# Where the causal mask is added: in the matmul group by TensorE, or in place by VectorE

## What is computed

```python
z = jnp.einsum('bhqd,bhkd->bhqk', qi, k).astype(jnp.float32) * scale
mask = key_pos[None, :] < qpos[:, None]
log_beta = jax.nn.log_sigmoid(z)
log_1m = jnp.where(mask, jax.nn.log_sigmoid(-z), 0.0)
after = lax.cumsum(log_1m, axis=3, reverse=True) - log_1m
a = jnp.where(mask, jnp.exp(log_beta + after), 0.0)
```

## Time and profile before

| | us |
|---|---|
| median of three runs | 1707.56 (1707.22 to 1708.33) |
| the profiled execution | 1705.47 |
| its span | 1703.8 |
| PE busy | 1684.4 (99%) |
| DVE busy | 970.5 (57%) |
| ACT busy | 738.5 (43%) |
| POOL busy | 220.3 (13%) |
| granted PE clock | nine tenths or more in all 40 slices, mean 0.999 |

### The profile page before, as it was taken

One profiled execution on the slowest core, in us unless ns is written; L12 is line 12 of the kernel. 1 busy time (PEld: TensorE's weight loads), 2 busy tenths in 40 slices (PEclk: granted clock), 3 DMA queues, 4 the chain that ended last, 5 costly groups with the idle time before them and its releaser, 6 DMA issues.

```text
span 1703.8 us, 22202 instructions
## 1 busy us (share of the span) xinstructions
PE 1684.4 (99%) x7651; PEld 1391.6 (82%) x7651; DVE 970.5 (57%) x1180; ACT 738.5 (43%) x1033; POOL 220.3 (13%) x204
## 2 busy tenths in 40 slices
PE   7999999999999999999999999999999999999998
PEld 6788888888888888888877888888888888888887
DVE  6787776544555434434658877755545543444344
ACT  5677676433333223223346777763333432232231
POOL 3243221000130000000333233200002100000000
PEclk9999999999999999999999999999999999999999
DMA  6232323333333333333343222223333333333333
GB/s 174 75 93 81 98 63 92 88 93 92 105 92 94 98 99 95 91 98 98 111 120 92 75 86 86 87 68 100 91 98 99 97 93 95 98 98 90 96 98 111
DMA packets 307416, 162.19 MB, mean 95 GB/s; under 512 B 5424, under 2 KB 303528, under 8 KB 307368
## 3 DMA queue, kind: packets, MB, share of 16 engines
q1 hardware_dynamic: 305064, 157.37, 31.5%
q10 hardware_dynamic: 2304, 4.20, 0.7%
HBM read 155.25 MB, written 2.10 MB: 92 GB/s over the span
## 4 chain that ended last, share of the span: by engine, by line
PE 95%; DVE 1%; ACT 1%; DVEq 1%; issue 0%; DMA 0%; POOL 0%; ACTq 0%; SPq 0%; POOLq 0%
PE bank L525 29%; PE bank L529 28%; PE bank L526 28%; PE z L598 2%; PE z L526 1%; PE z L525 1%; PE z L529 1%; PE z L571 1%; PE z L572 1%; PE misc L614 1%; PE misc L612 1%; DVEq L1595 0%; DMA gates<-in_x 0%; DVE w_lo L1192 0%; PE z L576 0%
## 5 line engine op out<-in xcount | busy, mean ns | idle before, releaser
L525 PE MATMUL bank<-xg_hi,w_hi 128*128 128x512 f32 x1584 | 622.7, 393 | 1.3 <-DVE xg_lo L1600 1.3
L526 PE MATMUL bank<-xg_lo,w_hi 128*128 128x512 f32 x1584 | 617.9, 390 | 0.0
L834 ACT ACTIVATE w_hi<-raw 128x1024 fp32r<-128x1024 f32 (+1 forms) x296 | 305.5, 1035 | 558.3 <-DMA raw<-in_w_gate_up 226.9
L1192 DVE TENSOR_TENSOR w_lo<-raw,w_hi 128x1024 fp32r<-128x1024 f32 (+1 forms) x296 | 391.2, 1324 | 38.0 <-ACT w_hi L834 22.1
L529 PE MATMUL bank<-xg_hi,w_lo 128*128 128x512 f32 x1584 | 392.3, 390 | 0.0
L525 PEld LDWEIGHTS bank<-xg_hi,w_hi 128*128 128x128 f32 x1584 | 297.6, 188 | 63.9 <-DVE xg_lo L1600 1.8
L526 PEld LDWEIGHTS bank<-xg_lo,w_hi 128*128 128x128 f32 x1584 | 297.7, 188 | 61.8 <-issue 0.7
L529 PEld LDWEIGHTS bank<-xg_hi,w_lo 128*128 128x128 f32 x1584 | 297.5, 188 | 62.0 <-issue 0.5
L1197 DVE TENSOR_TENSOR S<-bank,rstd 128x512 f32<-128x512 f32 x152 | 104.9, 690 | 269.3 <-PE bank L529 268.7
L525 PE MATMUL bank<-mid_hi,w_hi 128*128 128x512 f32 x480 | 189.9, 396 | 0.0
L526 PE MATMUL bank<-mid_lo,w_hi 128*128 128x512 f32 x480 | 189.6, 395 | 0.0
(11 more groups left out here) (206 smaller groups left out, 1686.7 us busy)
## 6 DMA issues: line engine op xcount, KB each, us to landing
raw<-in_w_in SPq DMA_DIRECT2D x112, 512.0 KB, 3.8
raw<-in_w_gate_up SPq DMA_DIRECT2D x88, 512.0 KB, 3.8
raw<-in_w_down SPq DMA_DIRECT2D x48, 512.0 KB, 3.6
raw<-in_w_branch_out SPq DMA_DIRECT2D x16, 512.0 KB, 3.6
raw<-in_w_o SPq DMA_DIRECT2D x16, 512.0 KB, 3.5
raw<-in_w_branch_out SPq DMA_DIRECT2D x16, 256.0 KB, 2.7
gates<-in_x SPq DMA_DIRECT2D x4, 512.0 KB, 7.1
mix_hi<-yb_hi ACTq DMA_DIRECT2D x8, 256.0 KB, 2.3
```

The source lines that it names most:

```text
L525: mm(dst[:, :], wh[:, k0 + k, :], his[k], start=(k % per == 0), stop=False)
L526: mm(dst[:, :], wh[:, k0 + k, :], los[k], start=False, stop=False)
L834: af(w_hi[at.slot(c)][:, 0:kc, :], raw[at.slot(c)][:, 0:kc, :], ACT.Copy).then_inc(hi_done, 1)
L1192: tt(w[:, 0:kc, :], r[:, 0:kc, :], h[:, 0:kc, :].bitcast(F32), ALU.subtract).then_inc(lo_done, 1)
```

## The change

`scores` no longer runs the three mask matmuls. The last score matmul of each z tensor raises a new semaphore `z_raw`, and a new function `causal` on DVE waits for it, adds `mask_add` to the diagonal columns of z in PSUM and raises `z_done`. `mask_add` is stored as plain fp32.

```diff
-        mask_add = sb("mask_add", [P, P], F32R)
+        mask_add = sb("mask_add", [P, P])
...
                         mm(dst, k_both[:, e, ks], q_twice[:, e, qs], start=(n == 0), stop=False, skip_group_check=True)
-                        mm(dst, k_both[:, e, ks], q_lo[:, e, qs], start=False, stop=False, skip_group_check=True)
-
-                    first = [Z_AT[i] // P for i in blocks]
-                    dst = z[g][:, :].rearrange("p (b q) -> p b q", q=P)[:, first[0]::(first[-1] - first[0]) or NT, :]
-                    mm(dst, ident_r[:, :], mask_add[:, :].rearrange("p (a q) -> p a q", a=1).broadcast_to([P, len(first), P]),
-                       start=False, stop=True, skip_group_check=True).then_inc(z_done, 1)
+                        last = mm(dst, k_both[:, e, ks], q_lo[:, e, qs], start=False, stop=(i == blocks[-1]),
+                                  skip_group_check=True)
+                    last.then_inc(z_raw, 1)
...
+            def causal(h3):
+
+                for g, blocks in Z_BLOCKS:
+                    dve.wait_ge(z_raw, h3 + (g + 1))
+                    first = [Z_AT[i] // P for i in blocks]
+                    diag = z[g][:, :].rearrange("p (b q) -> p b q", q=P)[:, first[0]::(first[-1] - first[0]) or NT, :]
+                    tt(diag, diag, mask_add[:, :].rearrange("p (a q) -> p a q", a=1).broadcast_to([P, len(first), P]),
+                       ALU.add).then_inc(z_done, 1)
+
...
                         yc_add(l * 8 + j * 2, 0)
+                        causal(h3 + 3)
                         softplus_sum(h3 + 3)
...
                     yc_add(l * 8 + j * 2, 0)
+                    causal(h3 + 3)
                     softplus_sum(h3 + 3)
...
                     yc_add(l * 8 + (j * 2 + 1), 1)
+                    causal(h3 + 6)
                     yc_rest(l * 8 + (j * 2 + 1), j, 1)
...
+                causal(l * 24)
                 with dve.Fori(0, PAIRS - 1) as j:
```

More of the change, by code:

```diff
@@ L265, in build @@
         slab_in = sem("slab_in")
+        z_raw = sem("z_raw")
         z_done = sem("z_done")
```

## The result

| | before | after |
|---|---|---|
| median of five runs | 1707.56 us (1707.22 to 1708.55) | 1715.71 us (1714.29 to 1716.69) |
| ratio to before, 95% interval | | 1.0046 (1.0035 to 1.0058) |
| the profiled execution | 1705.47 us | 1714.29 us |
| its span | 1703.8 us | 1712.6 us |

The kernel became 8.15 us slower. The forecast was 1713.0 us, 5.4 us slower, with a range up to 1717. Direction and range held; a third of the slowdown wasn't in the sum, and the result lies just above the forecast's own narrower range (1711 to 1715.5). Of the nine executions of the kernel without a mask, further down, one took 4357.55 us for no known reason, and the ratio leaves it out.

The account below looks back on a forecast made before the run. PE was taken to bound the kernel, busy 1684.4 of 1703.8 us. Waits of 8.6 us less 3.2 us of kept savings gave +5.4 us (+2.7 a layer): 1713.0 us, range 1706 to 1717.

Parts of the forecast that it names:

- The first piece of the mask: DVE's first 128-column addition in each call, which ACT's Abs waits for: 0.28 us, bounds 0.15 and 0.69.
- The rival of dear pieces: Writing back to PSUM makes the first piece cost 0.69 us, four times a layer: 1716.3 us, chance 0.14.
- The first pair's Abs: In a layer's first pair, Abs starts about 86.42, 2.2 us later, behind DVE's last weight split and first addition.
- the head squares: PE's matmuls on Q's squares in a layer's first pair, waiting for POOL without room: 2.2 us late.
- The middle of the pair: In each loop pair, head 1's Abs waits behind `yc_add`, 2.1 us later; PE then waits at `mix` and attend.
- The saving: PE time won by removing three mask matmuls from one `scores` call: 0.40 us; eight of 16 kept, 3.2 us.
- The rival of cheap masks: A mask matmul costs its columns alone, 0.23 us a call: 1714.4 us, chance 0.10.
- The last pair: A layer's last pair has no key norm and 2.5 us of room at attend: both 0.40 us savings kept.
- the first pair's attend: Attend of head 1 in a layer's first pair: chain 3.1 us late, less 1.0 of room, so 2.1 late.
- The second rival: Delays in the middle of pairs are absorbed, only a layer's first pair waits: 1706.4 us, chance 0.13.

Follow-up runs that it names:

- kernel without a mask: The kernel before with its 48 mask matmuls left out and nothing in their place, so scores are unmasked: 1702.29 us, ratio 0.9974.
- whole squares of K: POOL squares all 512 columns of K; the changed kernel with only 128 of them squared took 1712.04 us, ratio 1.0023.
- The curve: Loop-pair time against Abs's distance behind `yc_half` across kernels: 56.15 us at 0.73, 56.85 at 1.87 (additions ahead of `yc_add`, 1705.87 us), 57.73 at 2.75.
- both places early: The changed kernel with a layer's first additions moved up behind `layer_norm(3)` and head 1's ahead of `split_lo(at, 6)` on DVE: 1702.44 us, ratio 0.9975.
- only the middle early: The changed kernel with only head 1's additions, in the middle of a loop pair, moved up ahead of `split_lo(at, 6)`: 1707.39 us, ratio 1.0006.

## Why the prediction was right, and where its size was off

- **The first piece of the mask** at 0.28 us: 0.294. The rival of dear pieces was wrong, although its 1716.3 us lay nearest to the result. A right number for a wrong reason: its 0.69 us for a piece is in no trace.
- **The first pair's Abs** at 86.42 and the head squares 2.2 us late: 86.42 and 2.18, and moving the additions up took the wait away.
- **The middle of the pair**: Abs 2.1 us late, 2.13 measured; `mix` 0.6 and attend 1.1 late against the pair's start. Counted against attend of head 0 (163.96, where it was 160.97, so 2.99 late), `mix` at 178.94 is 3.71 - 2.99 = 0.72 late and attend of head 1 4.13 - 2.99 = 1.14. The waits stand in the first pair too, where the prediction had named only the second and third, and together they are 1.13 us, where it said about 1.5. What was missed at attend are 0.1 us behind the wait: the first matmul, which overlaps its successor where PE runs on, steps 0.33 us instead of 0.23 (136.28 to 136.61 in after, 133.02 to 133.25 before). With it a loop pair costs 1.14 + 0.10 - 0.37 = 0.87.
- **The saving** of 0.40 us a call: 0.35 to 0.37, between the bounds of 0.23 and 0.45. The four that count in a layer bring 0.1 to 0.2 us less than forecast. The rival of cheap masks (0.23) was wrong. The Trainium skill's page (TensorE: Matmul & The Clock Gate, Back-to-back issue gap), from which the estimate of 221 ns came, gives its cycles for a matmul by itself, and says that such a figure is too low for narrow matmuls that each load weights. The traces agree with that: no mask against before gives 0.35 us a call.
- **The last pair**: no wait, both savings kept, as forecast.
- **The term that was mis-sized** is the first pair's attend, forecast 2.1 and measured 3.26 us late. The step reads "so the chain starts 1.0 late. With 2.1 that makes 3.1". It took ACT's start of the norm for what holds the chain, and every duration unchanged from the trace of before. DVE's first norm step did start 1.0 late, at 104.37 instead of 103.39. But the end of the norm doesn't hang on that start: it comes 6.8 us behind the head squares in every kernel with whole squares of K, and these were 2.18 late. The step took 1.78 instead of 0.68 us, and `s_lo` ahead of it 3.30 instead of 4.10. So the norm ended 2.1 late, and Abs of head 1 started at 110.65 in place of 106.43, 4.2 late and not 3.1. The prediction's own numbers show the overlap: the squares of K, moved by 2.2, end at 103.19 + 2.2 = 105.4, and the step, moved by 1.0, starts at 104.4.

```profile
101.14 3.30 DVE L1228 TENSOR_TENSOR s_lo<-t_s,s_hi 128x512 fp32r<-128x512 f32 x3
```

```profile
110.65 1.36 ACT L874 ACTIVATE t_s<-z 128x512 f32<-128x512 f32 x3 [2.16 <-DVE z L1211]
```

```profile
106.43 1.36 ACT L876 ACTIVATE t_s<-z 128x512 f32<-128x512 f32 x3
```

The first two lines are of after, the third of before. This is 1.1 us for each layer, 2.2 of the 3.4 us by which the span's 8.8 exceed the sum of 5.4. The rest is the smaller saving and the 0.1 us behind the wait at attend.

In the trace of before there was a sign of it. DVE's `s_lo` just ahead:

```profile
99.36 4.10 DVE L1221 TENSOR_TENSOR s_lo<-t_s,s_hi 128x512 fp32r<-128x512 f32 x3 [0.32 <-ACT s_hi L896]
```

It took 4.10 us for three tiles while POOL squared K, where head 1's three take 1.62 in the second pair. The Trainium skill says the same as a rule (GPSIMD Engine Reference, Specifications): VectorE and GpSimd share their SBUF interfaces, and DVE instructions with two SBUF inputs are one of the two kinds that it names for contention. L1200 has two, `N` and `conv_in`, and the traces agree: 0.68 us alone, 1.78 under POOL.

The second rival, that only the first pair waits, was to give 1706.4 us, and its own condition decides it: below 0.6 us of delay nothing waits. The curve shows some 0.4 us absorbed and the rest passed on.

## What to carry to other kernels

An operation moved from the engine that bounds the kernel to one that is half idle is worth what its *position* in the new engine's list allows: here the same 48 additions lose 8.2 us in one place and win 4.9 in another, and the time of the last instruction ahead of them, in the trace of before, told the delay within 0.1 us in both places. Follow every semaphore that the moved step raises to the engine that bounds the kernel, and count the room there in tenths of a microsecond. When a chain is shifted, lay its new times over the other engines' lists too: a step that took 0.7 us alone took 1.8 where it fell beside POOL. And before a part of a delay is taken off as room, look at what the end of the step follows, and not only its start.

## What the runs showed of the hardware

PE's clock can fall after a wait of about 2 us, in some places and not in others. In the trace of before the granted clock has no low stretch behind the 1.96 us wait for `k_both`. In that of after it has one behind the same wait in layer 0, in that of the kernel with both places early one behind it in layer 1. In the kernel with only the middle early, one stands behind the new 2.43 us wait at the head squares in layer 0, while in layer 1 of after there is none behind a wait of 2.38 us at the same place. PE in the kernel with only the middle early:

```profile
101.14 0.79 PE L620 MATMUL misc<-sq_hi,head_ones 128*128 128x512 f32 x1 [2.43 <-POOL sq_lo L448]
101.73 0.63 PE L621 MATMUL misc<-sq_lo,head_ones 128*128 128x512 f32 x1
102.16 0.63 PE L526 MATMUL bank<-xg_hi,w_hi 128*128 128x512 f32 x1
102.58 0.63 PE L527 MATMUL bank<-xg_lo,w_hi 128*128 128x512 f32 x1
```

The same kernel by windows (us; PE, PEld, DVE, ACT and POOL busy, each with its instructions; granted clock; DMA share, GB/s):

```profile
102.00:104.00 2.00, 2.00 (x6) 1.54 (x6) 2.00 (x3) 1.37 (x3) 1.45 (x2) 0.51 0.00 0
104.00:106.00 2.00, 2.00 (x10) 1.61 (x9) 2.00 (x3) 1.93 (x3) 1.86 (x2) 1.00 0.00 0
```

A granted clock of 0.51 is the lower level, 1.2 of 2.4 GHz. A matmul of 512 columns steps by 0.42 us there and by 0.23 behind it. By the starts of the matmuls the stretch costs some 1.3 us, on top of the wait of 2.43. Such stretches are a likely source of the scatter of this kernel: its mean granted clock is 0.998 in the six executions up to 1707.61 us, 0.997 in the three from 1708.22 to 1709.78, and 0.995 in that of 1712.04. No run here separates it. Where one lies ahead of another wait it costs nothing: in layer 0 of after it is made up at the head squares, whose wait is 0.85 us there and 2.38 in layer 1.
